# Attention by pairs of heads: plain fp32 scores and weighted values in two groups of the array, projection in half tiles

## The reference, cut to what matters

```python
u = rms_norm(h, g_pre) @ w_in          # 1024 x 8320
# attention, for each head and each block of 128 queries:
z = q_blk @ k.T * HEAD_DIM ** -0.5
strict = s_pos < t_pos
log_1mb = where(strict, log_sigmoid(-z), 0)
suffix = cumsum(log_1mb, reverse=True) - log_1mb
attn = where(strict, exp(log_sigmoid(z) + suffix), 0)
y_b = (attn @ v) * silu(g_sb)
```

## Time and profile before

| | |
|---|---|
| time of the runs shown | 4020.99, 4027.18, 4037.97 us, median 4027.18 |
| span of the profiled execution, first to last instruction | 4052.5 us, of which 20.17 us at the end are the last entry of the chain, in which no work runs; no other time is given for this execution |
| PE busy | 3707.0 us, 91% |
| DVE, ACT, POOL busy | 1952.6, 1470.6, 389.8 us |
| mean granted TensorE clock | 0.920 |

### The profile page before, as it was taken

The page is one execution under the profiler, slowest core; times in us unless marked ns, Lnnn a source line. Parts: engine busy times, 40 slices in busy tenths (PEclk is TensorE's granted clock), DMA queues, the critical chain, the costliest instruction groups (busy, mean ns, idle before and its releaser), DMA issues.

```text
span 4052.5 us, 52239 instructions
## 1 busy us (share of the span) xinstructions
PE 3707.0 (91%) x18161; PEld 2939.6 (73%) x18161; DVE 1952.6 (48%) x3416; ACT 1470.6 (36%) x2784; POOL 389.8 (10%) x491
## 2 busy tenths in 40 slices
PE   6999999999999799998989998999977898989997
PEld 5777777777777577777767777777755686878786
DVE  3264564565565544444545444455544325442444
ACT  4164464465455332222222222222222224333433
POOL 2000000000000011111111111111111000010001
PEclk9999999999999998898989988899975699999999
DMA  3212212212212211011111111111000233343322
GB/s 123 89 40 73 67 36 72 67 39 72 67 36 74 63 42 38 31 43 45 32 45 45 43 34 41 34 43 45 30 22 10 91 127 115 104 141 115 125 94 83
DMA packets 217289, 257.27 MB, mean 63 GB/s; under 512 B 12061, under 2 KB 146302, under 8 KB 214782
## 3 DMA queue, kind: packets, MB, share of 16 engines
q1 hardware_dynamic: 200878, 199.84, 15.4%
q0 software_dynamic: 16208, 54.68, 3.9%
HBM read 203.03 MB, written 51.45 MB: 63 GB/s over the span
## 4 chain that ended last, share of the span: by engine, by line
PE 78%; DVE 10%; issue 6%; ACT 4%; DMA 2%; DVEq 0%; POOL 0%; ACTq 0%; SPq 0%; POOLq 0%
PE ps L422 31%; PE ps L1563 17%; PE ps L1486 4%; PE ps L1493 4%; PE ps L1364 3%; PE ps L1390 3%; PE ps L1375 3%; ACT tt L775 2%; PE ps L1525 2%; PE ps L1519 1%; PE ps L1517 1%; PE ps L1526 1%; PE ps L1444 1%; PE ps L1505 1%; PE ps L1464 1%
## 5 line engine op out<-in xcount | busy, mean ns | idle before, releaser
L422 PE MATMUL ps<-xh,wh 128*128 128x512 f32 x2080 | 736.8, 437 | 32.9 <-DVE wl L400 32.9
L422 PE MATMUL ps<-xl,wh 128*128 128x512 f32 x2080 | 681.2, 410 | 0.0
L422 PE MATMUL ps<-xh,wl 128*128 128x512 f32 x2080 | 673.9, 406 | 0.0
L422 PEld LDWEIGHTS ps<-xh,wh 128*128 128x128 f32 x2080 | 384.6, 199 | 159.8 <-issue 66.7
L422 PEld LDWEIGHTS ps<-xl,wh 128*128 128x128 f32 x2080 | 414.7, 199 | 95.7
L422 PEld LDWEIGHTS ps<-xh,wl 128*128 128x128 f32 x2080 | 412.9, 199 | 95.5
L396 ACT ACTIVATE wh<-w_raw 128x512 fp32r<-128x512 f32 x260 | 162.1, 629 | 715.3 <-PE ps L422 711.1
L1244 DVE TENSOR_TENSOR vl<-v_raw,vh 128x1024 fp32r<-128x1024 f32 x136 | 166.6, 1225 | 434.3 <-ACT vh L900 434.1
L400 DVE TENSOR_TENSOR wl<-w_raw,wh 128x512 fp32r<-128x512 f32 x260 | 178.1, 690 | 387.0 <-ACT wh L396 374.1
L900 ACT ACTIVATE vh<-v_raw 128x1024 fp32r<-128x1024 f32 x136 | 144.2, 1060 | 467.1 <-PE ps L1563 466.7
L623 POOL TENSOR_TENSOR nb<-ld,m_r 128x512 f32<-128x512 f32 x160 | 217.2, 1370 | 831.5 <-DVE ld L1162 479.4
(11 more groups left out here) (237 smaller groups left out, 5436.2 us busy)
## 6 DMA issues: line engine op xcount, KB each, us to landing
w_raw<-in_w_in SPq DMA_DIRECT2D x260, 256.0 KB, 2.9
u_t<-u_stage SPq DMA_DIRECT2D x130, 256.0 KB, 2.1
v_raw<-in_w_out SPq DMA_DIRECT2D x64, 512.0 KB, 3.8
v_raw<-in_w_plg SPq DMA_DIRECT2D x64, 512.0 KB, 3.8
x_in<-in_x SPq DMA_DIRECT2D x8, 1024.0 KB, 10.8
m_in<-mix_t SPq DMA_DIRECT2D x16, 512.0 KB, 3.9
x_res<-in_x SPq DMA_DIRECT2D x8, 1024.0 KB, 4.9
layer_out<-rows POOLq DMA_DIRECT2D x32, 256.0 KB, 3.0
```

Of the source, the lines that this page charges most:

```text
L422: mm = pe.matmul(banks[2 * par + t][:, :], wt[:, q % 2, k % QK], xt[:, k, t * HALF:(t + 1) * HALF], start=(k == 0 and n == 0), stop=(k == ...
```

## The change

**Units.** A step now covers both heads of a pair: 12 steps (Q, b) instead of 24 units. Two banks hold the scores of a step (3 and 4, or 5 and 6). The ACT and DVE instructions of a step work on both heads at once, on up to 2 x 512 columns.

**Scores and values.** q, k, v and the weights are no longer split: scores are one plain fp32 matmul for each head, on partitions 0 to 63 and 64 to 127 (two row groups), and values one plain fp32 matmul for each head with 64 columns of v (two column groups), into the two halves of bank 7. The splits of q, k, v and of the weights `pah`, `pal` go. The scale of q moves into the evacuation of its panel. The suffix sums stay as they are, in fp32r. Slot t: scores of t, filler, suffix sums of t-1, filler, values of t-1.

**Projection in half tiles.** `half_tile` does three matmuls for one half of the tokens; in a quarter first four contraction steps for one half, then four for the other (in the last quarter the second half first). The first half of a panel has two banks (0 and 1), the second one bank (2), whose evacuation by DVE now comes after half tile 28 of 32. Filler is counted in half tiles, 128 in a group.

**Weights.** In the attention stage the split weights have four buffers and quarter c + 3 is split when c quarters are done; in the RWKV stage two buffers, and quarter c + 1 when c are done, also over the border of a group (the last attention group and the last group with filler have lists of their own, which change over or stop). `store_panel` of a panel now comes in SP's program in the second quarter of the panel but one behind it.

**Loads.** q, k and v of the next pair are loaded before the end of the current one (`sb_load`), into tiles of their own or `r_t`.

```diff
-                kh = sb("kh", [P, S], F32R, ca)
-                vth = sb("vth", [P, TB, P], F32R, ca)
+                wh_b = sb("wh_b", [P, 2, QK, P], F32R, ca)
+                q_t = sb("q_t", [P, S], F32, ca)
+                e_t = sb("e_t", [P, 2, 2, HALF], F32, ca)
...
-        UNITS = [(Q, e, b) for Q in range(2) for e in range(2) for b in range(4 * Q + 3, -1, -1)]
+        UNITS = [(Q, b) for Q in range(2) for b in range(4 * Q + 3, -1, -1)]
...
-        PRE_V, PRE, SLOTS = 10, 15, NU + 4
+        SB_DEPTH, RW_DEPTH = 4, 2
+        PRE_V, PRE, SLOTS, GROUP = 6, 12, NU + 1, 128
...
+        def scores_us(a):
+            return 2 * max(0.213, (HALF - a) / 1200)
+        wish = [3.0 + (7.0 * (HALF - lo[t]) / HALF if t < NU else 1.0) for t in range(SLOTS)]
+        stretch = ((GROUP - PRE) * 0.68 + sum(work)) / sum(wish)
+        room = [max(1.0, stretch * w - k) for w, k in zip(wish, work)]
...
         def group_io(sp, cols, p_, before):
+            late = [before[0], before[1], cols[0], cols[1]]
             for j in range(16):
                 load_quarter(sp, cols[j // 4], p_ + j // 4, j % 4)
-                if j % 4 == 2:
-                    col = cols[j // 4 - 1] if j >= 4 else before
-                    if col is not None:
-                        store_panel(sp, col, p_ + j // 4 - 1)
+                if j % 4 == 1:
+                    store_panel(sp, late[j // 4], p_ + j // 4 - 2)
...
+        def panel_hi(dve, p_, par, scale):
+            dve.wait_ge(s_p1, p_ + 1)
             need(dve, s_ust[1], 16 * p_)
...
+        def half_tile(pe, p_, par, q, s, depth):
+            t, kk = (s // 4) ^ (q == 3), s % 4
+            k = q * QK + kk
+            if s == 0:
+                pe.wait_ge(s_wl, 4 * p_ + q + 1)
+            if k == 0 and t == 0:
                 need(pe, s_ulo, p_ - 1)
+            if k == 0 and t == 1:
+                need(pe, s_uhi, p_)
+            bank = banks[par] if t == 0 else banks[2]
+            for n, (wt, xt) in enumerate(((whs, xh), (whs, xl), (wls, xh))):
+                mm = pe.matmul(bank[:, :], wt[q % depth][:, kk], xt[:, k, t * HALF:(t + 1) * HALF],
+                               start=(k == 0 and n == 0), stop=(k == KT - 1 and n == 2))
+            if q == 3 and s == 3:
+                mm.then_inc(s_p1, 1)
...
-            return 32 * h + FILL[POINTS[k - 1]], 32 * h + FILL[point]
+            return 64 * h + 2 * FILL[POINTS[k - 1]], 64 * h + 2 * FILL[point]
...
+        SPLITS = {4: {c: (c + 3, 4) for c in range(1, 17)},
+                  2: {c: (c + 1, 2) for c in range(1, 17)}}
+        def follow_dve(dve, p_, a, b, kind, scale=1.0):
+            for j in range(a + 1, b + 1):
+                if j % 32 == 28:
+                    panel_hi(dve, p_ + j // 32, (1 + j // 32) % 2, scale if j == 28 else 1.0)
+                if j % 8 == 0 and j // 8 in SPLITS[kind]:
+                    c, depth = SPLITS[kind][j // 8]
+                    split_low(dve, p_ + c // 4, c % 4, depth)
...
-                        for m, (kt, qt) in enumerate(((kh, qh), (kh, ql), (kl, qh))):
-                            mm = pe.matmul(banks[4 + n % 3][:, lo[n]:], kt[h_, b * P:(b + 1) * P],
-                                           qt[h_, Q * HALF + lo[n]:(Q + 1) * HALF], start=(m == 0), stop=(m == 2))
+                        if n >= 2:
+                            pe.wait_ge(s_ex, U + n - 1)
+                        for e in range(2):
+                            h_ = slice(e * HD, e * HD + HD)
+                            mm = pe.matmul(banks[3 + 2 * (n % 2) + e][:, lo[n]:], k_t[h_, b * P:(b + 1) * P],
+                                           q_t[h_, Q * HALF + lo[n]:(Q + 1) * HALF], start=True, stop=True)
...
+                        pe.wait_ge(s_ex, U + n + 1)
+                        for e in range(2):
+                            h_ = slice(e * HD, e * HD + HD)
+                            mm = pe.matmul(banks[7][h_, lo[n]:], vt[:, b, h_], e_t[:, n % 2, e, lo[n]:],
+                                           start=first[n], stop=last[n], skip_group_check=True)
```

More of the change, by code:

```diff
@@ L195, in layer_kernel @@
         s_wused = sem("s_wused")
+        s_p1 = sem("s_p1")
         s_ulo = sem("s_ulo")
@@ L353, in layer_kernel, with suffix_us @@
         RW0 = N0 + 4 * NPAIR
[L355 to L363, removed]
+        def scores_us(a):
+            return 2 * max(0.213, (HALF - a) / 1200)
+        def suffix_us(n):
+            one = max(0.213, (HALF - lo[n] + 32) / 2400)
+            return 2 * ((2 if first[n] else 4) * one + (0.213 if diag[n] else 0))
+        work = [(scores_us(lo[t]) if t < NU else 0) + (suffix_us(t - 1) + scores_us(lo[t - 1]) if t else 0)
+                for t in range(SLOTS)]
+        wish = [3.0 + (7.0 * (HALF - lo[t]) / HALF if t < NU else 1.0) for t in range(SLOTS)]
+        stretch = ((GROUP - PRE) * 0.68 + sum(work)) / sum(wish)
+        room = [max(1.0, stretch * w - k) for w, k in zip(wish, work)]
         def tiles_by(t, part):
@@ L368, in tiles_by @@
                 return PRE
-            if t == SLOTS - 1:
-                return 64
-            return PRE + (64 - PRE) * (3 * sum(room[:t]) + (part + 1) * room[t]) // (3 * sum(room[:-1]))
+            if t == SLOTS - 1 and part == 1:
+                return GROUP
+            return PRE + int((GROUP - PRE) * (sum(room[:t]) + (part + 1) * room[t] / 2) / sum(room))
         def load_quarter(sp, col, p_, q):
@@ L591, in _ @@
+                    pool.wait_ge(s_y, 2 * i + Q + 2)
+                    pool.dma_start(mix_t[bass.ds(rows, P), Q * HALF:(Q + 1) * HALF], gt[:, 1]).then_inc(s_mst, 16)
+            for t in range(2):
+                pool.wait_ge(s_ust[t], 16 * 4)
+            sb_load(0)
+            sb_io(0, True)
+            with pool.Fori(1, NPAIR - 1) as i:
+                sb_io(i, True)
+            sb_io(NPAIR - 1, False)
+            pool.wait_ge(s_mst, 32 * NPAIR)
             pool.dma_start(m_r[:, :, :], mask_d[:, :].rearrange("p (m t) -> p m t", t=P)).then_inc(s_mld, 16)
@@ L1366, in sb_pe @@
-                        mm.then_inc(s_z, 1)
-                    tiles(pe, p_, tiles_by(t - 1, 2), tiles_by(t, 0))
-                    n = t - 3
-                    if 0 <= n < NU:
-                        Q, e, b = UNITS[n]
-                        if first[n]:
-                            need(pe, s_y, 4 * i + chain[n])
-                        pe.wait_ge(s_al, U + n + 1)
-                        for m, (vt, at) in enumerate(((vth, pah), (vth, pal), (vtl, pah))):
-                            mm = pe.matmul(banks[7][:, lo[n]:], vt[:, b], at[:, n % 2, lo[n]:],
-                                           start=(first[n] and m == 0), stop=(last[n] and m == 2), skip_group_check=True)
-                        mm.then_inc(s_pv, 1)
```

374 lines of the change are left out of this document (173 added, 201 removed).

## The result

The changed kernel takes 3860.77 us, the median of 4 runs (3848.85 to 3871.55), beside 4024.09 us for the kernel before in 4 runs on the same chip (4018.19 to 4037.97). The ratio is 0.9589 [0.9563, 0.9615], 4.1% faster. The forecast was 3922 us, 2.6% faster, and its range ended at 3868.

The account below looks back on a forecast made before the run. The prediction took PE, busy 91% of the span, as the bound. Scores and values -97, attention waits -25 and RWKV +17 gave -105 us, from 4027 to 3922 us, range 3868 to 3985.

Parts of the forecast that it names:

- (a): Attention stage: PE's wait for the q, k, v splits goes; with (b) 25 us in eight pairs.
- (b): Attention stage: a chain's first values no longer wait for DVE's bank 7 read; with (a) 25 us in eight pairs.
- the steps wait: Rival, chance 0.12: attention steps wait for ACT and DVE; at 0.8 us a step 77 us, giving 3999.
- the groups take turns: Rival, chance 0.08: column groups take turns at 512 columns, 7.7 us a pair more, 61 in all, giving 3983.
- the 35 us of loss in the overlap: Scores and values: at about 0.78 of ideal overlap, 4.3 us a pair more, 35 in all, result 3956.
- (d): Attention slot 4: values newly wait for ACT's exp, 0.6 us; with slot 12, 0.7 a pair, 6 us.
- (c): Attention group borders: the first tile's wait shrinks, but PE takes 2.1 us at a loop's turn; 6 us gained.
- The new wait in RWKV: RWKV stage: DVE's evacuation stands still until the store of the panel before lands; 7 x 4.7 = +33 us.
- No late store: Rival, chance 0.12: the store lands before it's wanted, RWKV gives 31 us instead of costing 17: 3874.
- The turn term: RWKV loop's turn: 3 us sooner at six turns, -18; a split falling into the second half's c4, +6.
- the other half starts 0.6 sooner: RWKV stage: the half not at the loop's turn starts sooner, 7 x 0.6 = -4 us.
- The evacuation's part: RWKV: DVE's 0.68 us evacuation leaves two critical places, before the Gram masks and the next half's start, and is hidden.

Follow-up runs that it names:

- full_values: Changed kernel with each head's values matmul taking all 128 columns of v and writing all of bank 7, without column groups: 3890.86 us.
- waits_first: Changed kernel with PE's two waits at the end of an RWKV half put ahead of the last filler: 3865.15 us (1 run).
- before_split_m: Kernel before, with DVE's splits and evacuations that fall into c4 to c7 moved to point m: 4024.07 us beside 4030.76.
- late_store: Changed kernel with the second store of each two issued one quarter later in SP's program: 3894.91 us.
- border: Changed kernel with the splits of a group's first two quarters back at the head of the RWKV loop body: 3857.41 us.
- evac_32: Changed kernel with DVE's evacuation of a panel back at its end, half tile 32 instead of 28: 3884.24 us.
- apart: Changed kernel with one half tile of filler between a step's values and the next slot's scores: 3891.33 us.
- end_wait: Changed kernel with one more, always met wait at the end of PE's program of an attention pair: 3851.79 us.

## Why the prediction was right and wrong

**Right.** PE sets the pace and the change takes work from it; both new forms run in groups at the same time; three changes of form serve a step; waits (a) and (b) go; slot 4 waits for the exp. A full step was forecast at 2.32 us and takes 2.27. ACT and DVE keep up (no wait for `rl`), so the attention steps are not bound by latency. With that and full_values, the rivals by which the steps wait or the groups take turns are out, and the 35 us of loss in the overlap that the forecast weighed aren't there either.

Where the 58 us between 105 and 163 are:

| term | forecast | found | from |
|---|---|---|---|
| scores and values | -97 | -109 | pair without waits 142.2 to 128.65 |
| waits (a) to (d) | -25 | -41 | waits of PE, 5.5 to 0.41 a pair |
| lower clock in the attention stage | 0 | -12 | pair 1.5 over the undisturbed one before |
| rest of head and turn | 0 | +4 | stage 1380.6 to 1222.2 |
| RWKV | +17 | about -5 | what is left of the medians |

**Scores and values** were mis-sized: 13.6 us a pair, not 12.1. The full steps account for 6 x 0.05 = 0.3 of the 1.5 missing. (The forecast's 0.79 for 256 columns is 0.84 by its own sum, which is 0.1 a pair.) The rest is in "columns/2.4 GHz + 0.014 us for narrower ones", as the timeline of PE in the kernel before shows at 128 and at 256 columns:

```profile
346.04 0.27 PE L1364 MATMUL ps<-ql,kh 64*128 64x128 f32 x1
346.15 0.27 PE L1364 MATMUL ps<-qh,kl 64*128 64x128 f32 x1
...
350.89 0.28 PE L1364 MATMUL ps<-ql,kh 64*128 64x256 f32 x1
351.01 0.27 PE L1364 MATMUL ps<-qh,kl 64*128 64x256 f32 x1
```

In a row of such matmuls, a split one of 128 columns takes 0.11 us, no less than one of 256 (0.12), where I had 0.067. A step of 128 columns had twelve of them, so the change takes 12 x 0.045 = 0.54 us more out of each, 1.1 in the two of a pair. With the full steps that is 1.4 of the 1.5 us. The row was there to be read before.

**Wait (c), the border, failed.** The step was "at a loop's turn PE itself takes 2.1 us, as in the RWKV loop". The trace of after has no gap at any border. I carried the 2.1 us from the RWKV loop to a place where they don't occur. There PE's instruction stream is held by a late wait just ahead of the branch, and waits_first shows that this makes almost half of the gap; the cause of the rest stays open. Worth 2.0 us at each of six borders, 12 in all. Wait (d) was put at 0.7 a pair and is 0.41.

**The clock in the attention stage was left out.** I counted waits at their length. The pairs of before average 1.5 us over the undisturbed ones, with 41 us at the lower level against 16 after. The profiles of all the kernels with the new attention stage have 13 to 17 us there, that of before_split_m, with the old one, 30. So the difference belongs to the stage, but that the waits gone are the reason is argued, not shown.

**The new wait in RWKV failed,** by the step "in the RWKV stage that is the split at 1746.63, directly ahead of the evacuation". That split is of the next panel's first quarter. The buffer that the load ahead of the store needs is freed by the one of the last quarter, which is done at half of the panel, not at three quarters, since the RWKV stage splits one quarter ahead. So the stores are long out, 11.5 us ahead. late_store makes the wait real and costs 27 to 43 us, of which the waits of PE are 17. The rival *No late store* had the cause right with a chance of 0.12. Its 3874 came near by two errors against each other: it lacks 36 us of the attention stage, and its -31 in RWKV, the bound with 4 us at each turn, was about -5. An RWKV pair was forecast to get 2 to 3 us longer. From the first start of L1417 to that of the seventh pair it averages 224.4 us after and 228.9 before, and most of that difference is the clock.

**The turn term (-18 + 6) is nothing in sum,** since its second part was mis-sized. Border gives the turn back, and the preparation of the first halves gets 14 to 19 us longer, so the 18 hold. But the new wait in c4 was put at its length, 6 x 1 us, and is worth 11 to 16, most of it by the clock. The 4 us of "the other half starts 0.6 sooner" aren't there: that preparation takes 165 us before and after. The evacuation's part holds at the Gram masks, and evac_32 costs 13 to 32 us in all.

## What to carry to other kernels

Before a wait is forecast from the order of a queue, write down which buffer each load needs and which instruction frees it: one quarter of a panel decided between +33 us and nothing. A gap at one loop's turn can't be carried to another loop as the price of the branch; look at what holds the engine's stream just ahead of it. Where the clock falls in a stage, look for PE's short waits there and try to remove them even if their sum is small, but measure it in the whole, since the same edit gave 54 to 60 us in one kernel and 7 in another. And compare stretches between the same instructions over several profiles: the stage's length alone hid the effect of border and of before_split_m.

## What the runs showed of the hardware

- In a row, a split matmul of 128 columns takes as long as one of 256, 0.11 to 0.12 us, while the plain fp32 values of 128 columns don't show such a floor (0.37 us with the change of form, from 320.88 to 321.25 in the trace of after, where the forecast's sum gives 0.42).
- Two plain fp32 matmuls in two column groups take 1.01 us at 512 columns with the change of form, and as full-width matmuls 1.81. The Trainium skill (TensorE: Matmul & The Clock Gate, Measured speedup vs the span model) has a speedup of 2.38 for three column groups and 3.07 for four row groups, about 0.78 of the ideal; for two groups these rows show the ideal, with only the changes of form beside it.
- Each change of form costs 0.19 us (a full step, 2.27 less 2 x 0.853, for three) to 0.24 (apart), and going from the column form straight to the row form is one change.
- A wait of PE that is already met costs nothing that can be seen (end_wait: pair 129.08 against 129.06). At the RWKV loop's turn PE stands for 1.7 us on average, and for 1.0 when the late waits come 12 matmuls earlier; at the attention loop's turn there is no gap.
- A wait of PE of 1.0 us between the chunk steps lengthens them by some 2 to 4 us, mostly through PE's clock. Taking out thirteen made one program 54 to 60 us faster (PE's busy time in the stage 41 to 68 us less); taking out seven made another 7 us faster in the median, with 20 us less in the chunk steps of its profile.
- A store of 256 KB lands after 3.3 us in the median in the changed kernel, where nearly every one is issued right behind a load. In the kernel before, 30 such stores took 3.6, the 100 others 2.1.
